# Eight delta-rule heads: projection moved into the second mixer's projection stage, core as a pipeline of three heads

## The reference, cut to what matters

```python
h = rmsnorm(x, norm_g) * (1 + scale) + shift          # and hc for the context
u, uc = h @ w_in, hc @ w_in
ya = gdn_mixer(...)      # 8 heads of 128, the gated delta rule, both directions
yb = rwkv_mixer(...)     # 16 heads of 64 (8 pairs), both directions
x = x + gate * (concat(ya, yb) @ w_out)
# gdn_prep
qkv = silu(centred_dwconv(u[:3 * 1024], conv_w))      # width 5
q, k, v = l2norm(q) * 128 ** -0.5, l2norm(k), v;  z = u[3 * 1024:4 * 1024]
g = -exp(a_log) * softplus(gates + dt_bias);  beta = sigmoid(...)
# gated_delta_chunked, per head and direction, chunks in order
lmat = strict(kb @ k.T * decay);  tmat = inverse(eye + lmat)
u_, wk = tmat @ (v * beta), tmat @ (kb * exp(g));  attn = tril(q @ k.T * decay)
v_new = u_ - wk @ state
o = (q * exp(g)) @ state + attn @ v_new
state = state * exp(g_last) + k_tail.T @ v_new
# gdn_output
y = rmsnorm(o, norm_g) * silu(z)
```

## Time and profile before

| | |
|---|---|
| median of 3 runs | 4770.96 us (4765.27 to 4775.19) |
| the profiled execution | 4768.8 us, its span 4766.9 us |
| mean granted TensorE clock | 0.919 |
| busy in the span | PE 3907.7 us (82%), DVE 2177.3 (46%), ACT 1053.5 (22%), POOL 1251.4 (26%) |
| HBM | 337.43 MB read, 49.50 MB written |

### The profile page before, as it was taken

One profiled execution on the slowest core, in us unless ns is written; L12 is line 12 of the kernel. 1 busy time (PEld: TensorE's weight loads), 2 busy tenths in 40 slices (PEclk: granted clock), 3 DMA queues, 4 the chain that ended last, 5 costly groups with the idle time before them and its releaser, 6 DMA issues. The chain is left out here.

```text
span 4766.9 us, 58834 instructions
## 1 busy us (share of the span) xinstructions
PE 3907.7 (82%) x21386; PEld 3079.3 (65%) x21386; DVE 2177.3 (46%) x3882; ACT 1053.5 (22%) x1823; POOL 1251.4 (26%) x706
## 2 busy tenths in 40 slices
PE   7778888888984799997688888888596977887697
PEld 2247556655763688886688878778474755675375
DVE  0354553455357425665454554555402267763202
ACT  1111121112111235554122122122102112220201
POOL 0034425333544000000000000000064644555063
PEclk9889899989987899998799999999798988998899
DMA  7223223221331114442211111111332211112131
GB/s 277 97 81 107 95 61 101 92 90 59 120 93 46 35 63 142 138 132 93 72 33 46 35 46 36 34 45 33 113 118 90 86 53 57 62 62 66 53 111 70
DMA packets 256743, 386.60 MB, mean 81 GB/s; under 512 B 142577, under 2 KB 174849, under 8 KB 252097
## 3 DMA queue, kind: packets, MB, share of 16 engines
q1 hardware_dynamic: 243728, 360.14, 24.1%
q10 hardware_dynamic: 12848, 24.24, 1.4%
HBM read 337.43 MB, written 49.50 MB: 81 GB/s over the span
## 5 line engine op out<-in xcount | busy, mean ns | idle before, releaser
L1004 PE MATMUL pjl<-high,w_high 128*128 128x512 f32 x960 | 394.1, 410 | 195.3 <-DVE arena L2602 48.6
L478 PE MATMUL pjl<-hT,ring 128*128 128x512 f32 x1024 | 511.9, 604 | 20.7 <-DMA ring<-in_w_g 12.6
L987 POOL TENSOR_TENSOR w_high<-ring_o,cst 128x1024 fp32r<-128x1024 f32 x152 | 303.4, 1996 | 567.8 <-PE pjl L1006 398.3
L621 POOL TENSOR_TENSOR arena<-arena,RP 128x1024 f32<-128x1024 f32 x128 | 249.2, 1947 | 600.6 <-DMA arena<-in_w_ada 590.1
L1005 PE MATMUL pjl<-low,w_high 128*128 128x512 f32 x960 | 384.2, 400 | 0.0
L1006 PE MATMUL pjl<-high,w_low 128*128 128x512 f32 x960 | 383.1, 399 | 0.0
L989 POOL TENSOR_TENSOR w_low<-ring_o,w_high 128x1024 fp32r<-128x1024 f32 x152 | 377.5, 2484 | 11.9
L1004 PEld LDWEIGHTS pjl<-high,w_high 128*128 128x128 f32 x960 | 187.2, 195 | 251.0 <-issue 166.9
L2128 POOL MEMSET unused<- 128x1 f32 x1 | 0.1, 99 | 1129.1 <-POOLq L187 1129.1
L2592 DVE SCALAR_TENSOR_TENSOR arena<-arena 128x512 f32<-128x512 f32 x232 | 251.8, 1085 | 7.8
L478 PEld LDWEIGHTS pjl<-hT,ring 128*128 128x128 f32 x1024 | 180.3, 195 | 100.4 <-issue 67.9
(11 more groups left out here) (471 smaller groups left out, 8693.6 us busy)
## 6 DMA issues: line engine op xcount, KB each, us to landing
arena<-in_w_ada SPq DMA_DIRECT2D x128, 512.0 KB, 3.9
ring<-in_w_lr SPq DMA_DIRECT2D x72, 512.0 KB, 4.2
arena<-in_w_ada SPq DMA_DIRECT2D x32, 1024.0 KB, 6.8
ring<-in_w_g SPq DMA_DIRECT2D x64, 512.0 KB, 4.4
ring_o<-in_w_out SPq DMA_DIRECT2D x64, 512.0 KB, 3.7
ring_o<-in_w SPq DMA_DIRECT2D x64, 512.0 KB, 3.6
arena_r<-rk_d SPq DMA_DIRECT2D x128, 192.0 KB, 3.5
rk_d<-arena_p SPq DMA_DIRECT2D x72, 192.0 KB, 1.9
```

Source lines behind the costliest of these rows:

```text
L478: last = pe.matmul(lat, ring[:, s, kk % HK], hT[:, kk, 0:LAT], start=kk == 0, stop=kk == KT - 1)
L621: pool.tensor_tensor(w, w, c, ALU.mult).then_inc(S["g_lm"], 1)
L987: pool.tensor_tensor(h, w, one, ALU.mult).then_inc(S[done + "h"], 1)
L1004: pe.matmul(lat, wh[:, c], ah, start=kk == 0, stop=False)
```

## The change

- `phase_gates` no longer projects head 0 (nor clears its buffers). It computes `exp(g)` rows (two ACT exponentials, four DVE products) and stores them as a third set of `gate_rows`.
- `phase_gdn` moves behind `phase_rwkv`, and its projection and preparation leave it for `phase_proj`, which gets 8 more periods, one for each head, behind the 8 pairs. A head's four tiles are projected as the pairs' are: three fp32r products, weights split by ACT and DVE. In a head's period PE has the next head's tiles; the first head's tiles fill the last pair's period. ACT does the convolution's first tap, the sigmoids, the squares; DVE the other four taps, silu, the products with norms, beta and decay. The norms are made as columns (`head_norms`: ten matmuls of one column each), turned to rows, stored to HBM and loaded back broadcast over partitions. SP stores each head's results (12 DMAs, 3.4 MB) to `ga_d`, `gv_d` and `gs_d`. The buffers overlay those of the pairs, so that the first head waits until the pairs' last stores have landed, and ACT's first tap of the next head waits until the current head's stores have landed (`q_st`).
- The late groups of `w_ada` leave POOL and `phase_gdn`. In the heads' periods POOL issues 256 DMAs of 256 KB, one for each group and k, into two slots (`late`), each as soon as DVE has used the slot; DVE multiplies and accumulates, one instruction of 512 columns for each (`later`), in bursts of 8, 4, 5, 5, 5 and 5 between the steps of a head. The last head has no next head, and takes its 32 in one row (8 and 24).
- The core of a head is now three overlapping parts, as in `phase_rwkv`: `start` of head m+2 (decay matrices, k k^T, q k^T, the 15-step solve of 16x16 blocks), `invert` of head m+1 (three doubling levels in place of seven, then the transposed keys and values), and the scan of head m, whose 18 gaps hold a piece of each (`fill`). Head 0's `start` and head 0's `invert` beside head 1's `start` come ahead of the first scan. The heads are written out and not looped. Decay matrices are made by four DVE instructions and three of ACT, in place of 24 small DVE ones.

```diff
-    raw = carve(3, GT + 4)
-    zraw = carve(LAT)
...
-            for n in range(8):
-                sp.wait_ge(w_used, half + n - RING + 1)
-                sp.dma_start(e["ring"][:, n % RING], io["w_g"][n // 2, :, n % 2 * HK:(n % 2 + 1) * HK]).then_inc(e["w_loaded"][n % RING], 16)
...
+            sp.wait_ge(S["b_eg"], 2)
+            for d in range(2):
+                sp.dma_start(gate_rows[2, d], eg[d][8 * d:8 * d + 8]).then_inc(S["b_out"], 16)
+            sp.wait_ge(S["b_out"], 96)
...
-            for j in range(4):
-                if j:
-                    pe.wait_ge(S["b_raw"], (0, 1, 3, 5)[j])
-                project(pe, e, 0, j, loads(half), pj[0][:, 0:LAT], pj[2][:, 0:CTX] if j in (1, 2) else None)
...
+            streams_stored(pool)
+            for x in range(32 * GH):
+                if x >= 2:
+                    pool.wait_ge(S["q_lu"], x - 1)
+                pool.dma_start(late[:, x % 2], io["w_ada"][8 + x // 16, :, x % 16]).then_inc(S[f"q_lw{x % 2}"], 16)
...
+            def head(h):
+
+                t, more, after = 40 + 4 * h, h < GH - 1, h < GH - 2
+                sp.wait_ge(S["q_silu"], 3 * h + 3)
+                both(gv_d[h], qkv[:, 2], "q_vs")
+                sp.wait_ge(S["q_zz"], h + 1)
+                sp.dma_start(gs_d[h, :, GS_N - 12 - LAT:GS_N - 12], gz).then_inc(S["q_zs"], 16)
+                if more:
+                    halves_of(t, 4, 6)
+                sp.wait_ge(S["q_pre"], h + 1)
+                store_head(h)
+                if more:
+                    halves_of(t, 6, 8)
+                    sp.wait_ge(S["q_st"], 9 * 16 * (h + 1))
+                    rows_of(h + 1)
+                    if after:
+                        halves_of(t + 4, 0, 3)
+                    norms_of(h + 1)
+                    if after:
+                        halves_of(t + 4, 3, 4)
...
+            def head(h):
+
+                t, more = 40 + 4 * h, h < GH - 1
+                if more:
+                    pe.wait_ge(S["p_ev"], t - 1)
+                    tile(t, 0, False)
+                if h:
+                    share(2 * h - 1)
+                if more:
+                    pe.wait_ge(S["p_ev"], t)
+                    tile(t, 1, True)
+                    pe.wait_ge(S["p_ev"], t + 1)
+                    tile(t, 2, True)
+                    head_norms(h + 1)
+                share(2 * h)
+                if more:
+                    pe.wait_ge(S["p_ev"], t + 2)
+                    tile(t, 3, False, (0,))
+                    turn_norms(h + 1)
+                    tile(t, 3, False, (1,))
+                else:
+                    share(2 * h + 1)
...
+            def next_head(h, t, n, between):
+
+                weights(n + 4)
+                if h:
+                    act.wait_ge(S["q_zz"], h)
+                else:
+                    act.wait_ge(S["q_v0"], 1)
+                head_raw(t, 0)
+                weights(n + 5)
+                if between:
+                    between()
+                    head_raw(t + 1, 1)
+                    weights(n + 7)
+                    streams_stored(act)
+                else:
+                    act.wait_ge(S["q_st"], 9 * 16 * h)
+                head_tap(h, 0)
+                head_sigmoid(h, 0)
+                head_square(h, 0)
+                if not between:
+                    weights(n + 6)
+                    head_raw(t + 1, 1)
+                    weights(n + 7)
+                head_tap(h, 1)
+                head_sigmoid(h, 1)
+                head_square(h, 1)
+                weights(n + 8)
+                head_raw(t + 2, 2)
+                if h:
+                    act.wait_ge(S["q_vs"], 32 * h)
+                head_tap(h, 2)
+                act.wait_ge(S["q_ss"], h + 1)
+                act.activation(ncol, col, ACT.Sqrt, bias=eps[:]).then_inc(S["q_nc"], 1)
+                head_sigmoid(h, 2)
+                act.wait_ge(S["q_tr"], h + 1)
+                act.activation(rowsb[0:10], nrT[0:10], ACT.Copy).then_inc(S["q_rw"], 1)
+                weights(n + 9)
+                head_raw(t + 3, 3)
+                act.wait_ge(S["q_silu"], 3 * h + 3)
+                act.activation(gsg[:, 0:LAT], zraw, ACT.Sigmoid).then_inc(S["q_sig"], 1)
...
+            def later(count):
+
+                for _ in range(count):
+                    x = done[0]
+                    g, k = x // 16, x % 16
+                    which = 0 if g < 4 else 2
+                    c, a = csk[:, 3 * k + which:3 * k + which + 1], acc[:, g % 2]
+                    dve.wait_ge(S[f"q_lw{x % 2}"], x // 2 * 16 + 16)
+                    if k == 0:
+                        if g >= 2:
+                            dve.wait_ge(S["q_sh"], g - 1)
+                        dve.tensor_scalar(a, late[:, x % 2], c, None, ALU.mult).then_inc(S["q_lu"], 1)
+                    else:
+                        dve.wait_ge(S["q_lu"], x)
+                        dve.scalar_tensor_tensor(a, late[:, x % 2], c, a, ALU.mult, ALU.add).then_inc(S["q_lu"], 1)
+                    done[0] += 1
...
+            def next_head(h, m, count):
+
+                head_conv(h, 0)
+                later(count)
+                head_silu(h, 0)
+                if h:
+                    weights(m + 6)
+                head_conv(h, 1)
+                later(count)
+                if h:
+                    weights(m + 7)
+                head_silu(h, 1)
+                later(count)
+                weights(m + 8)
+                head_conv(h, 2)
+                dve.wait_ge(S["q_nc"], h + 1)
+                dve.reciprocal(ncol, ncol).then_inc(S["q_rc"], 1)
+                later(count)
+                head_silu(h, 2)
+                weights(m + 9)
+                dve.wait_ge(S["q_sig"], 4 * h + 4)
+                if h:
+                    dve.wait_ge(S["q_zs"], 16 * h)
+                dve.tensor_tensor(gz, zraw, gsg[:, 0:LAT], ALU.mult).then_inc(S["q_zz"], 1)
+
+            def head(h):
+
+                m = 16 + 8 * (PAIRS + h)
+                more = h < GH - 1
+                if more:
+                    weights(m + 2)
+                    weights(m + 3)
+                dve.wait_ge(S["q_nl"], 48 * (h + 1))
+                link(dve.tensor_tensor(qkv[:, 1], qkv[:, 1], sqk, ALU.mult))
+                dve.scalar_tensor_tensor(qkv[:, 0, 0:LAT], qkv[:, 0, 0:LAT], float(P) ** -0.5, sqq, ALU.mult, ALU.mult)
+                dve.wait_ge(S["q_rows"], 64 * (h + 1))
+                for d in range(2):
+                    link(dve.tensor_tensor(KB[:, d], KB[:, d], qkv[:, 1], ALU.mult))
+                for d in range(2):
+                    dve.tensor_tensor(KBG[:, d], KB[:, d], EG[:, d], ALU.mult)
+                dve.wait_ge(S["q_zs"], 16 * (h + 1))
+                for d in range(2):
+                    end = 0 if d else P - 1
+                    dve.tensor_tensor(QG[:, d], qkv[:, 0, 0:LAT], EG[:, d, 0:LAT], ALU.mult)
+                    dve.tensor_copy(egl[:, d, 0:4], EG[:, d, end:LAT:P])
+                    last = dve.tensor_copy(egl[:, d, 4:6], EG[:, d, GC + end:GT:P])
+                last.then_inc(S["q_pre"], 1)
+                if h:
+                    keep_share(2 * h - 1)
+                later(8)
+                if more:
+                    weights(m + 4)
+                    weights(m + 5)
+                    later(4)
+                    next_head(h + 1, m, 5)
+                else:
+                    later(24)
+                keep_share(2 * h)
...
+            def fill(m, n):
+
+                if m >= 1:
+                    norm(m - 1, n)
+                if m + 1 < GH and n < 3:
+                    invert(m + 1, n)
+                if m + 2 < GH:
+                    start(m + 2, n)
+                if m + 1 < GH and n >= 3:
+                    invert(m + 1, n)
+
+            def scan(m):
+
+                if m:
+                    dve.wait_ge(S["g_s"], m * 14)
+                for d in range(2):
+                    dve.memset(St[0][:, d], 0.0).then_inc(S["g_s"], 1)
+                dve.wait_ge(S["g_lc"], m * 16 + 16)
+                for j in range(UN):
+                    old, new = St[j % 2], St[1 - j % 2]
+                    for d in range(2):
+                        dve.wait_ge(S["g_w"], m * 12 + 2 * j + d + 1)
+                        dve.tensor_tensor(W[:, d], bV[m % 2][:, d, G_ORDER[d][j]], xu[d][:, 0:P], ALU.subtract).then_inc(S["g_wc"], 1)
+                    fill(m, 3 * j)
+                    fill(m, 3 * j + 1)
...
-PHASES = [(phase_mod, "a"), (phase_gates, "b"), (phase_gdn, "g"), (phase_split, "s"), (phase_proj, "p"), (phase_rwkv, "r"),
+PHASES = [(phase_mod, "a"), (phase_gates, "b"), (phase_split, "s"), (phase_proj, "pq"), (phase_rwkv, "r"), (phase_gdn, "g"),
           (phase_out, "o"), (phase_two, "nz")]
 SEMS = """a_par a_x a_sig a_sq a_ss a_eps a_rt a_scl a_xn a_h a_hc a_cs a_mc a_d a_used a_row a_turn a_w0 a_w1 a_w2 a_w3 a_w4 a_w5 a_w6 a_w7
```

(42 more changed lines are left out.)

1054 lines of the change are left out of this document (545 added, 509 removed).

## The result

The changed kernel takes 4799.53 us (median of 4 runs, 4790.26 to 4802.22) against 4768.69 us before (median of 4, 4765.27 to 4775.19): a ratio of 1.006, 95% interval 1.0041 to 1.0078. It is slower, by 31 us or 0.6%; 4818 us (+1.0%) was forecast. The profiled execution has a span of 4794.5 us.

What follows compares the result with a forecast made beforehand. The old delta-rule stage was held bound by a head's serial chain, not by an engine's busy time. 4768.8 - 1320 - 39 + 838 + 569 gave 4818 us (+1.0%), own range 4775 to 4870, wider range 4700 to 4920.

Steps and rivals of the forecast that it cites:

- The stage account: Whole kernel by stages: delta-rule stage -1320 us, gates -39, projection stage +838, new core +569.
- the signs named: Changed profile: `gv_d` stores 102 us apart, core outputs 62, the first 170 to 180 after its start, gates' stage 75 us.
- The period: Projection stage, one head: DVE sets the distance of heads, 102 us, seven such periods making 714.
- Late waits: DVE in a head's period: waiting for late weight loads makes the 32 pieces cost 63 us in place of 25.
- PE hides entirely: Heads' periods: PE's 55 us of a head's tiles lie wholly within DVE's period, PE busy about half of it.
- L: Late slots: time from DVE's release of a slot to the landed next piece, taken as 3.9 us.
- rival 1: Late loads: the round trip is short, 3.0 us, 93 us less, 4725 us in all; chance 0.36.
- The count of rounds: Late pieces: DVE waits a round trip 12.5 times a head and 15 in the last, 103 in all.
- The new core: Delta-rule core, three heads overlapped: 110 us ahead of the first scan, 62 a full scan, 569 in all.
- rival 3: New core: scans run at 69.6 us and more as the second mixer's, +46 to +90, about 4885 us; chance 0.07.
- Rival 4: Heads' periods: late pieces never make DVE wait, a head costs 62 us, 4493 us in all; chance 0.04.
- rival 2: Late loads: round trip long, 5.0 us, +113, 4931 us; GpSimd-issued DMAs starving while DVE holds the port would add; chance 0.13.

Runs made afterwards that it cites:

- e1: Changed kernel with the late weight groups left out whole, no loads and two clears for the 256 DVE pieces: 4454.3 us.
- e8: Changed kernel with only 8 columns of each of the six large stores behind a head's products, head 0 storing all: 4779.1 us.
- e9: Changed kernel with only 8 columns of a head's four row loads (beta and exp(g)) for all heads but head 0, stores whole: 4765.4 us.
- e11: Changed kernel with both the thinned stores and the thinned row loads of a head: 4742.7 us.
- e6: Changed kernel with four small waited-for clears on POOL ahead of the issue of every late load: 4854.6 us.
- e7: Changed kernel with each late load but the first two bringing 256 of its 512 columns, DVE computing on all 512: 4743.6 us.
- e2: Changed kernel with all 256 DVE pieces computed, but each late slot loaded only once, at the start: 4504.0 us.
- e3: Changed kernel with the bursts of late pieces broken up, one or two pieces behind nearly every other DVE instruction, still two slots: 4672.5 us.
- e5: Changed kernel with four late slots and the pieces spread between other DVE work: 4572.5 us, ratio 0.9593 to the kernel before.
- e10: e5 with the six pieces ahead of a head's stores moved right behind them: 4587.5 us, 0.9625 of the kernel before.
- e4: Changed kernel with four slots for the late pieces in place of two, the bursts kept: 4599.4 us.

## Why the prediction was right

**The stage account** held at every step: what goes from the gates, 102 us a head where 102.5 was measured, the last pair's +42 against +43. Nor did the work of the other stages change. Of the signs named, the stores into `gv_d` (102.9 us apart, 102 said) and the gates' stage (72.5 us, 75 said) came out; the first output of the new core came 194 us after its start, not 170 to 180.

**The period.** DVE's products, splits, convolutions and pieces came to 57 us in my sum and 53 in the trace (each instruction starts some 0.09 us before the one ahead of it ends). Late waits: 38 forecast, 42 measured; other waits 6.7 against (29.5 + 7.2) / 5 = 7.3. PE hides entirely, as said, though its own term was small: 55 us and busy for half of a period were forecast, it needs 60 when it is fed (e1, clock 0.98), and is busy for 67 us, 65%, at the clock of 0.79. That cost nothing here.

**L was mis-sized, and a term was missing.** The step that put L at 3.9 us took the 3.2 us of the 256 KB row from SP, two hops of 0.2 and 0.3 for traffic. In the quiet last head L is 3.3. With that rival 1 was near: 103 x 0.6 = 62 us less, about 4756; and DVE's work of 53 us in place of 57 takes another 28 off. What kept the sum whole is the term that I had folded into 0.3 us: the landings beside a head's own rows, stores and weights, up to 9.9 us. Rounds of 4.0 us would give some 31 us of waits a head, and 42 were measured. e8, e9 and e11 give 7 us a head for rows and stores, 50 us in seven heads, and e11 leaves some 2 us a head beside the weights. Errors of 50 to 80 us in each direction cancelled. The forecast was right by mechanism and place; that the period came out at 102 against 102.5 was luck. The earlier trace rows had shown the 386 KB rows at 5.1 us, and I used them as the upper bound of L and not as what four of them do to a load behind them.

**The count of rounds** (12.5 a head, 15 in the last) was near: e6 gives 11.2 and 13, e7 7.4 / 0.6 = 12.3 and, with 68.2 us for its last head, 9.4 / 0.6, 15 to 16.

**Two slips without weight.** 4816.8 and the 2.2 us to the median make 4819, not 4818. And the 69 us of a head's projection in the kernel before come out as 74 if one goes by the earlier trace rows as the text says (4 x 16 x 4 x 0.23 + 2 x 16 x 4 x 0.115); nothing in the sum hangs on them.

**The new core** was forecast by its pieces, 110 + 6 x 62 + 48 + 39 = 569. DVE's clears that open the scans run from 2991.2 to 3359.5 for six full scans, 61.4 us each:

```profile
2991.21 0.30 DVE L863 MEMSET arena_r<- 128x128 f32 x2
...
3359.49 0.31 DVE L863 MEMSET arena_r<- 128x128 f32 x2
...
3400.36 0.30 DVE L863 MEMSET arena_r<- 128x128 f32 x2
```

The head is 108 us, the scan without a `start` 40.9 (48 forecast), the last one with norm and store 37.6 (39). Inside a full scan the six steps are 15.2, 12.7, 10.2, 10.2, 8.3 and 4.4 us long, from the differences at L869 in the scan opened at 3113: a serial head and gaps of 10, as in the sum, but a longer second gap and a shorter last. So rival 3 (69.6 and more) fell. Of the 14 us between forecast and core 2 are the head, 4 the six full scans, 7 the scan without a `start` and 1 the last.

**Rival 4** (the pieces never make DVE wait) stated 4493; with the waits taken out and the pieces kept, e2 gives 4504. The rival was wrong in its condition and nearly right in its price. **The bound of the page** in rival 1: the Trainium skill (DMA: Bandwidth & Descriptors, Anatomy of one DMA — SWDGE (gpsimd) path) gives 2.0 us plus bytes at 436 GB/s, by estimate 2.6 us for 256 KB and 2.3 for 128; the runs have 3.0 and 2.4, with two loads in flight. The level is near, the slope is twice as steep. Of the starving in rival 2 there is no sign: with DVE's pieces set between its other work in e3 the median landing stays 3.0, and through the longest of the waits looked at, 7.60 us in the changed kernel and 4.86 in e11, DVE did nothing at all.

**What the change did in all.** It saves 1321 us of the old stage and 41 in the gates, and pays 555 for the core with three heads overlapped and 837 for the projection. Of these 837 the late weights are 345 (4799.5 - 4454.3). With the late groups as cheap as e2 makes them, where the waits and the traffic of the loads are gone, the change would have gained some 265 us (4504 against 4769); their waits in two slots turn that into a loss of 31. e5, which computes everything, gains 196.

## What to carry to other kernels

A buffer of two slots whose reader takes pieces in bursts paid nearly a full round trip for every two pieces here, whatever the engine's busy share said (DVE worked for 53 us of 102): count rounds before bytes, and look at which other transfers are issued at that moment. Spreading the pieces between other work gained 127 us, four slots in place of two 200, both together 227: each of the two is worth more alone than on top of the other. When a wait is taken away, read the list of waits again before the next edit: in e5 the store chain and in e10 the loads stood where the old wait had been.

## What the runs showed of the hardware

**The granted clock follows PE's idle time.** In the changed kernel, between 1259 and 1340 (us, busy times, granted clock, DMA share, GB/s):

```profile
1259.00:1277.00 18.00, 17.96 (x95) 15.06 (x94) 13.08 (x22) 5.25 (x6) 0.54 (x1) 1.00 0.50 155
1277.00:1286.00 9.00, 8.77 (x51) 7.40 (x50) 2.16 (x3) 0.00 (x0) 2.14 (x4) 1.00 0.97 335
1286.00:1295.00 9.00, 0.22 (x1) 0.26 (x2) 4.51 (x6) 0.72 (x1) 2.14 (x4) 0.66 0.53 175
...
1320.00:1340.00 20.00, 0.51 (x3) 0.51 (x3) 11.81 (x14) 5.68 (x8) 3.37 (x7) 0.50 0.44 132
```

It is 1.00 (2.4 GHz) while PE works without a break, 0.66 over a stretch in which it stood, and 0.50 (1.2 GHz) over one of 20 us with next to no matmul. PE's busy time for the same tiles is 67 us a head there and 60 in e1.

**Loads in flight slow each other well below a full DMA share.** In the last head two loads of 256 KB in flight bring one every 2.0 us (131 GB/s) and land after 3.0 us (median); four in flight, in e4's last head, land after 3.3 us, and the stretch of 53 us moves 215 GB/s at a DMA share of 0.65. Whether more slots than four would still help was not tried.

**A load issued from POOL** takes 0.54 us of POOL and lands after 3.0 us, no later than the 256 KB load from SP in the earlier trace rows, 3.2.
